# The entry of a fused two-block kernel: modulation by column strips on the tensor engine, and four output groups started quarter by quarter

## The reference, cut to what matters

```python
c_act = jax.nn.silu(c)
mod = c_act @ w_ada[layer] + b_ada[layer]              # 2048 -> 12288
sh1, sc1, gt1, sh2, sc2, gt2 = jnp.split(mod[:, None, :], N_MOD, axis=-1)
h = rmsnorm(x, g_mix[layer]) * (1 + sc1) + sh1
x = x + (1 + gt1) * mixer(h, ...)                      # begins with proj = h @ w_in
h = rmsnorm(x, g_ffn[layer]) * (1 + sc2) + sh2
x = x + (1 + gt2) * conv_ffn(h, ...)
return rmsnorm(x, g_final)
```

## Time and profile before

| what | value |
|---|---|
| median of 3 runs | 2693.53 us (2693.23 to 2693.92) |
| the profiled execution | 2693.06 us |
| its span in the profile | 2691.3 us |
| PE busy | 2606.3 us, 97% of the span |
| DVE busy | 1934.7 us, 72% |
| ACT busy | 1223.7 us, 45% |
| mean granted clock of TensorE | 0.98 |

### The profile page before, as it was taken

How to read it: one execution, slowest core, us unless ns; L and a number is a source line. 1 busy time by engine, 2 the same in 40 slices (tenths; PEclk the granted TensorE clock), 3 DMA queues, 4 the chain that set the end, 5 groups by cost and what they waited for, 6 DMA issues and landing times.

```text
span 2691.3 us, 39482 instructions
## 1 busy us (share of the span) xinstructions
PE 2606.3 (97%) x14717; PEld 2277.7 (85%) x14717; DVE 1934.7 (72%) x2749; ACT 1223.7 (45%) x1595; POOL 118.1 (4%) x177
## 2 busy tenths in 40 slices
PE   5799999999998999999999999998999999999998
PEld 4788888888887888888888888886888888888887
DVE  6987778896888888855666658998676644566554
ACT  2144644444654655544555542004454433444443
POOL 0011121100010000000000000000000000000000
PEclk7699999999999999999999999999999999999999
DMA  9898688875776777755666544552666655666553
GB/s 362 305 299 256 218 249 268 272 222 157 231 259 214 254 247 248 234 188 188 189 189 191 188 158 147 150 155 84 199 180 188 191 189 188 188 188 190 187 185 133
DMA packets 494008, 560.50 MB, mean 208 GB/s; under 512 B 19384, under 2 KB 458937, under 8 KB 493625
## 3 DMA queue, kind: packets, MB, share of 16 engines
q1 hardware_dynamic: 474169, 488.50, 56.5%
q0 software_dynamic: 19712, 70.26, 8.4%
HBM read 553.45 MB, written 2.10 MB: 206 GB/s over the span
## 4 chain that ended last, share of the span: by engine, by line
PE 91%; DVE 5%; DMA 2%; issue 1%; ACT 1%; SPq 0%; ACTq 0%; DVEq 0%
PE ps L1665 53%; PE ps L1667 26%; PE ps L1981 8%; DMA att<-in_w_ada 2%; DVE wlo L976 1%; DVE tCDE L1099 1%; PE ms L1999 1%; PE ms L1716 0%; DVE att L1099 0%; DVE norm_rows L1080 0%; PE ms L1696 0%; PE ms L1739 0%; DVE norm_rows L1015 0%; DVE sq L1554 0%; DVE small L1269 0%
## 5 line engine op out<-in xcount | busy, mean ns | idle before, releaser
L976 DVE TENSOR_TENSOR wlo<-raw,whi 128x1024 fp32r<-128x1024 f32 x794 | 970.6, 1224 | 605.3 <-ACT whi L609 597.3
L1665 PE MATMUL ps<-xhl,whi 128*128 128x512 f32 x4352 | 1381.7, 399 | 16.5 <-DVE xhl L1563 7.3
L609 ACT CAST whi<-raw 128x1024 fp32r<-128x1024 f32 x794 | 831.0, 1050 | 1048.6 <-PE ps L1667 1025.1
L1667 PEld LDWEIGHTS ps<-xhl,wlo 128*128 128x128 f32 x4352 | 823.5, 189 | 195.4
L1667 PE MATMUL ps<-xhl,wlo 128*128 128x256 f32 x4352 | 860.2, 279 | 0.0
L1665 PEld LDWEIGHTS ps<-xhl,whi 128*128 128x128 f32 x4352 | 668.7, 190 | 21.2 <-issue 19.4
L1665 PE MATMUL ps<-ghl,whi 128*128 128x512 f32 x1024 | 319.5, 393 | 0.0
L1667 PEld LDWEIGHTS ps<-ghl,wlo 128*128 128x128 f32 x1024 | 192.2, 188 | 44.5
L1981 PE MATMUL ps<-xg,raw 128*128 128x256 f32 x1024 | 221.3, 379 | 0.0
L1665 PE MATMUL ps<-fhl,whi 128*128 128x512 f32 x704 | 219.3, 393 | 0.0
L1981 PEld LDWEIGHTS ps<-xg,raw 128*128 128x128 f32 x1024 | 194.5, 190 | 26.4
(11 more groups left out here) (263 smaller groups left out, 1447.5 us busy)
## 6 DMA issues: line engine op xcount, KB each, us to landing
raw<-in_w_in SPq DMA_DIRECT2D x176, 512.0 KB, 4.5
raw<-in_w_up SPq DMA_DIRECT2D x176, 512.0 KB, 3.9
ada<-in_w_ada POOLq DMA_DIRECT2D x128, 512.0 KB, 4.7
raw<-in_ffn_w_up SPq DMA_DIRECT2D x128, 512.0 KB, 3.8
raw<-in_ffn_w_down SPq DMA_DIRECT2D x128, 512.0 KB, 3.3
raw<-in_conv_w_pw SPq DMA_DIRECT2D x96, 512.0 KB, 3.8
raw<-in_w_down SPq DMA_DIRECT2D x88, 512.0 KB, 3.4
att<-in_w_ada SPq DMA_DIRECT2D x32, 1024.0 KB, 8.8
```

The source lines that it names most:

```text
L609: nc.scalar.copy(whi[t % SPL][:, :, :], raw[t % RAW][:, :, :]).then_inc(s_hi, 1)
L976: nc.vector.tensor_tensor(wlo[t % SPL][:, :, :], raw[t % RAW][:, :, :], whi[t % SPL][:, :, :].bitcast(F32), ALU.subtract).then_inc(s_lo, 1)
L1665: mm(o[:, m, :, :], whi[t % SPL][:, c, m * P:(m + 1) * P], x, start=first and c == 0, stop=last and c == KC - 1, skip_group_check=True)
L1667: ins = mm(o[:, m, 0, :], wlo[t % SPL][:, c, m * P:(m + 1) * P], x[:, 0, :], start=False, stop=last and c == KC - 1, skip_group_check=True)
```

## The change

Eight modulation groups are now multiplied wholly by PE. `silu(c)` is laid out as 16 blocks of 32 equal columns (`cact_strips`), and chunk j of a piece is multiplied with the block as the stationary operand, its 512 columns moving, into partitions 32j to 32j+31 of a bank: four products that use a quarter of the array's columns each. After four pieces ACT copies the bank (`rows_copied`), and `first_columns` turns it into columns and adds the four strips with a vector that has a one in each strip. DVE does no products any more. The pieces go through a ring of five 1 MB buffers. `x` is loaded first, and its squares are summed in the way of the later norms (`new_square`, `add_older`, `older_sum`, `newest_sum`).

The first 16 units (before: 8) are laid out anew: unit t holds 2 chunks by 512 columns, so that a quarter of four output groups is done as soon as quarter j of `h` is there. A block of a chunk and 256 columns is six products of 256 columns instead of two of 512 and two of 256, all into the same sum, so these four groups need no low copy. The other modulation pieces start later (`pieces_by`), and some background work is moved by four pieces or steps with them.

```diff
+FIRST_RING = 5
+STRIP = 32
+WIDE = 4
+EARLY = 4 * WIDE
+B_ANGLE = 9
...
-    return max(0, s - 2) + (s >= 4) + (s >= 7) + (s >= 10) - sum(s >= B_ROPE + 2 * k for k in range(4))
+    return max(0, s - 8) + sum(s >= 10 + 2 * k for k in range(5)) - sum(s >= B_ROPE + 2 * k for k in range(4))
...
# SP
+            def first_piece(n, q):
+
+                i = 4 * n + q
+                if i >= FIRST_RING:
+                    sp.wait_ge(s_firstmm, i - FIRST_RING + 1)
...
-            for q in (1, 2, 3):
-                first_quarter(0, q)
             x_in = A["x"].rearrange("b (c p) (h t) -> p (b c) h t", p=P, t=T)
...
-            first_quarter(0, 0)
+            for q in range(4):
+                first_piece(0, q)
+            for t in range(2):
+                first_weights(t)
+            first_piece(1, 0)
             sp.dma_start(posi, A["positions"]).then_inc(s_in[1], 16)
             load_vectors(sp, other_vecs, s_vin[1])
             sp.dma_start(cons[:, C_SW128:], A["consts"][:, C_SW128:]).then_inc(s_rest, 16)
+            units_behind = {(1, 3): (2, 3), (2, 3): (4, 5), (3, 3): (6, 7), (5, 1): (8, 9), (5, 3): (10, 11), (7, 1): (12, 13), (7, 3): (14, 15)}
             for n in range(1, ADA_START):
...
+                for q in range(1 if n == 1 else 0, 4):
+                    first_piece(n, q)
+                    for t in units_behind.get((n, q), ()):
+                        first_weights(t)
...
# ACT, after the eight copies of x
+            for i in range(DC // 2):
+                act.wait_ge(s_trx, i + 1)
+                new_square(0, i)
...
+            for t in range(4):
+                split_hi(0, t)
+            rows_copied(0)
...
-                square(i, i)
+            root(0)
...
+            rows_copied(7)
+            first_hi(3)
+            split_hi(0, 14)
+            split_hi(0, 15)
...
+                if t >= EARLY - 2 and t < EARLY:
+                    first_out(2 * (t - EARLY + 2))
...
# DVE
+            for j in range(1, 7):
+                add_older(0, j)
...
+            for t in range(4):
+                split_lo(0, t)
+            read_first(0)
+            root(0, EPS1, s_var2, 1)
+            read_first(1)
+            norm_first(0)
+            for j in range(1, 4):
+                read_first(2 * j)
+                split_lo(0, 4 * j)
+                split_lo(0, 4 * j + 1)
+                read_first(2 * j + 1)
+                norm_first(j)
+                split_lo(0, 4 * j + 2)
+                split_lo(0, 4 * j + 3)
...
# PE
+            def first_piece(n, q):
+
+                i = 4 * n + q
+                pe.wait_ge(s_adaring[i % FIRST_RING], 16 * (i // FIRST_RING + 1))
+                for j in range(4):
+                    ins = mm(row_bank(n)[STRIP * j:STRIP * (j + 1), :], cact_strips[:, 4 * q + j, :], ada_first[i % FIRST_RING][:, j, :],
+                             start=q == 0, stop=q == 3, skip_group_check=True)
+                ins.then_inc(s_firstmm, 1)
+
             def first_columns(n):
+                a = 4 * FIRST[n]
+                pe.wait_ge(s_rows, n + 1)
...
+                for m in range(4):
+                    ins = mm(bank_m[:, a + m:a + m + 1], first_rows[n % 2][:, P * m:P * (m + 1)], one_of_strip[:, 0:1], start=True, stop=True)
...
+            for q in range(4):
+                first_piece(0, q)
+            first_piece(1, 0)
...
-            first_modulation(0)
-            statistic(0)
+            first_columns(0)
             pe.wait_ge(s_posf, 1)
             mm(bank_o[:, T:2 * T], ones[0:1, :], posf, start=True, stop=True).then_inc(s_posb, 1)
+            older_sum(0)
+            newest_sum(0)
+            for q in range(1, 4):
+                first_piece(1, q)
...
+                for m in range(PC):
+                    for x in range(2):
+                        mm(ps[a][:, g, m, :], wh[:, m * P:(m + 1) * P], xhl[:, k, x, :], start=k + x + m == 0, stop=False, skip_group_check=True)
+                for m in range(PC):
+                    ins = mm(ps[a][:, g, m, :], wl[:, m * P:(m + 1) * P], xhl[:, k, 0, :], start=False, stop=k == DC - 1, skip_group_check=True)
...
             for n in range(2, ADA_START):
+                first_piece(n, 0)
+                first_columns(n - 1)
+                first_piece(n, 1)
+                if n >= 3:
+                    first_unit(2 * (n - 3))
+                first_piece(n, 2)
+                if n >= 3:
+                    first_unit(2 * (n - 3) + 1)
+                first_piece(n, 3)
+            first_chunk(10, 0)
+            first_columns(ADA_START - 1)
+            first_chunk(10, 1)
+            first_unit(11)
+            for a in range(2):
+                for g in range(2):
+                    for c in range(2):
+                        ins = first_block(12 + a, c, g)
+                    if g:
+                        ins.then_inc(s_used, 1 + a)
+                    for c in range(2):
+                        ins = first_block(14 + a, c, g)
+                    ins.then_inc(s_firstout, 1)
```

More of the change, by code:

```diff
@@ L98, in nth_split @@
     return t if t < T_PW1 else t - N_PW1
[L101 to L109, removed]
 def pieces_by(s):
-    return max(0, s - 2) + (s >= 4) + (s >= 7) + (s >= 10) - sum(s >= B_ROPE + 2 * k for k in range(4))
+    return max(0, s - 8) + sum(s >= 10 + 2 * k for k in range(5)) - sum(s >= B_ROPE + 2 * k for k in range(4))
 def swap_slot(r):
     return 8 + 2 * (r if r < 8 else r - 4)
-SWAPS_AT = {42: (0, 1), 43: (2, 3), 45: (4, 5), 46: (6, 7), 54: (8, 9), 56: (10, 11)}
+SWAPS_AT = {38: (0, 1), 39: (2, 3), 41: (4, 5), 42: (6, 7), 50: (8, 9), 52: (10, 11)}
 def low_nth(group):
@@ L310, in build @@
         s_cact = sem("c_activated")
-        s_adaring = [None] + [sem(f"first_modulation_landed{s}") for s in range(1, 4)]
+        s_adaring = [sem(f"first_modulation_landed{s}") for s in range(FIRST_RING)]
         s_adaland = [sem(f"modulation_landed{s}") for s in range(2)]
@@ L502, in _ @@
             sp.dma_start(cons[:, C_SW128:], A["consts"][:, C_SW128:]).then_inc(s_rest, 16)
+            units_behind = {(1, 3): (2, 3), (2, 3): (4, 5), (3, 3): (6, 7), (5, 1): (8, 9), (5, 3): (10, 11), (7, 1): (12, 13), (7, 3): (14, 15)}
             for n in range(1, ADA_START):
[L504 to L510, removed]
+                for q in range(1 if n == 1 else 0, 4):
+                    first_piece(n, q)
+                    for t in units_behind.get((n, q), ()):
+                        first_weights(t)
+            columns(EARLY, 24, w_in, 4 * CW)
             w_small = A["w_in"].rearrange("a (h c p) n -> (a h) p c n", p=P, c=DC // 2)
@@ L668, in first_hi, with first_out @@
                     nc.scalar.activation(xh[:, c, :], sq[:, c % 4, :], ACT.Identity, bias=mod[:, c:c + 1]).then_inc(s_nh, 1)
-            root(0)
+            rows_copied(1)
             first_hi(0)
[L672 to L678, removed]
+            rows_copied(2)
+            rows_copied(3)
+            split_hi(0, 4)
+            split_hi(0, 5)
+            first_hi(1)
+            split_hi(0, 6)
+            split_hi(0, 7)
+            rows_copied(4)
+            rows_copied(5)
+            split_hi(0, 8)
+            split_hi(0, 9)
+            first_hi(2)
+            split_hi(0, 10)
+            split_hi(0, 11)
+            rows_copied(6)
+            split_hi(0, 12)
+            split_hi(0, 13)
+            rows_copied(7)
+            first_hi(3)
+            split_hi(0, 14)
+            split_hi(0, 15)
+            act.sem_inc(s_low, WIDE)
+            def first_out(G):
+                act.wait_ge(s_firstout, G + 1)
+                nc.scalar.copy(att[:, 2 * G:2 * G + 2, :], ps[G // 2][:, G % 2, :, :]).then_inc(s_free[G // 2], 1)
             def background(s):
@@ L1774, in first_units @@
-            def first_units(q):
-                for k in range(2):
-                    if q == 0:
-                        pe.wait_ge(s_free[k], 1)
-                    rhs = from_x(H_QKV)
-                    unit(0, 2 * q + k, ps[k], lambda c: rhs(KC * q + c), q == 0, q == 3)
-            for n in range(2, ADA_START):
-                first_columns(n)
-                if n == 7:
-                    first_units(2)
-                first_modulation(n)
-                if n in (4, 5):
-                    first_units(n - 4)
@@ L1789, in _, with first_block @@
-            first_units(3)
+            def first_block(t, c, g):
+                k, a = 4 * (t // 4) + 2 * (t % 4 // 2) + c, t % 2
+                if k == 0 and g == 0:
+                    pe.wait_ge(s_free[a], 1)
+                pe.wait_ge(s_lo, RAW + t + 1)
+                pe.wait_ge(s_h, H_QKV + k + 1)
+                wh, wl = (wide(w[t % SPL])[:, c, CW * g:CW * (g + 1)] for w in (whi, wlo))
+                for m in range(PC):
[3 more added lines that the diff above has]
+                    ins = mm(ps[a][:, g, m, :], wl[:, m * P:(m + 1) * P], xhl[:, k, 0, :], start=False, stop=k == DC - 1, skip_group_check=True)
+                return ins
```

217 lines of the change are left out of this document (87 added, 130 removed).

## The result

The changed kernel takes 2700.86 us (median of 8, 2698.52 to 2704.84) where the one before takes 2693.95 beside it (8 runs, 2692.52 to 2696.43): a ratio of 1.0027, with an interval of 1.0018 to 1.0036. It is slower by some 7 us where 12 less were forecast. The profiled execution took 2701.23 us, its span is 2699.3.

What follows compares the result with a forecast made beforehand. It took the entry as bound by DVE and transfers together, PE mostly idle. 2693.06 - 16.1 (entry) + 3.5 (debts) + 1.0 (clock and strips) = 2681.5; the median 0.5 above, 2682 us; range 2669 to 2697.

Steps and rivals of the forecast that it cites:

- unit 16: End of the entry, from where both kernels issue the same products: PE begins it at 144.0 us, gain 16.1.
- the debts: At the top-64 search, late modulation pieces cost 3.5 us: 2.9 for steps 76 and 77, 0.6 for the next two.
- The transfers: Entry loads: 44.2 MB ahead of the last piece at about 405 GB/s, done at 115.3 us without the hole.
- the clock: Clock falling while PE waits in group 7, with going in and out of strips: 1.0 us lost (0 to 4).
- the strips: Entry pieces: four column strips run at once on PE, 0.86 plus 0.1 us a piece, hidden behind transfers.
- the hole: Near 43 to 50 us the queue empties, piece (2,2) waiting for its buffer: 7.0 us, 3.2 at full clock.
- second: Rival: entry strips overlap only as program order allows, 1.73 us a piece; 2694, no change; chance 0.12.
- third rivals: Rival: entry strips run one after another, 3.45 us a piece, so PE bounds the entry; 2731; chance 0.11.
- fourth rival: PE does not reach full clock from group 3 on: five groups, 35 us, 2717; chance 0.06.
- Steps 78 and 79: Late modulation pieces after the search meet DVE with slack: 0 to 2.9 us, taken as 0.6.
- The bank of unit 16: Unit 16 waits for copies behind the splits of unit 17: from 140.9, 1.04 + 1.22 + 0.6 and delays, to 144.0.
- first rival: Little of the losses comes, in the entry and steps 76 to 79: 2670, or 2676 for half; chance 0.16.

Runs made afterwards that it cites:

- e1: Changed kernel with its new 2-element tile made 128 bytes wide, so later tiles stand on multiples of 64 bytes again: 2694.18 us, ratio 1.0008.
- e2: Changed kernel with its new tile made 64 bytes wide, so later tiles stand on a multiple of 64 but not 128 bytes: 2691.50 us, ratio 0.9995.
- e9: Changed kernel with the new tile allocated last, so every other tile has its address of before: 2688.88 us, ratio 0.9986.
- e3: Kernel before with an unused 2-float tile ahead of `gain2`, moving the tiles behind it by 32 bytes: 2705.52 us, ratio 1.0042.
- e7: Kernel before with unused 2-float tiles ahead of `fhl` and `ghl` only, piece buffers left in place: 2700.25 us, ratio 1.0023.
- e11: Kernel before with an unused tile of 32 elements ahead of `gain2`, moving the tiles behind it by 128 bytes: 2696.53 us, ratio 1.0015.
- e12: Kernel before with `small` and an unused tile allocated ahead of `gain2`, moving the tiles behind by 256 bytes: 2693.32 us, ratio 1.0003.
- e5: Changed kernel with no modulation pieces in steps 73 to 77 and the last one at step 83: 2694.68 us, ratio 1.0005.
- e6: Changed kernel with ACT and DVE emptying the bank of unit 16 before they split units 17 and 18: 2698.73 us, ratio 1.0019.
- e10: Changed kernel with the tile allocated last, hole closed, pieces held back in steps 73 to 77, and bank copies first: 2672.24 us, ratio 0.9922.

## Why the prediction was wrong

**The step that failed** stands in its first paragraph: unit 16, "from where both kernels issue the same products". They are the same products, but not on the same addresses. The sum of the prediction holds no term for the stream behind the entry but the debts, and "The transfers" divides its 44.2 MB by 405 GB/s, the rate of the old addresses. One line of the diff, the new tile of two floats ahead of `gain2`, broke both: 0.03 to 0.04 us on 248 units, some 7 us, and 387 for 405 GB/s, 4.6 to 6.3 us at unit 16. It is shown from both sides, by taking the offset out of the change (e1, e2, e9) and by putting it alone into the kernel before (e3, e7, e11, e12).

**The sum, term by term**, against the profiled 2701.2, 19.7 above the forecast's 2681.5. Unit 16 is 10.9 late (154.87 for 144.0), the search is 2.4 above the 3.5 of the debts, the later units lose 7.2, and the lead shrinks by 0.6 between units 16 and 152. The 1.0 set aside for the clock is in the first of these, and 0.3 comes back behind the last product: 19.8. Of the 10.9, 6.3 go with the offset by the traces of the change and of e9. The other 4.6 are in e9 as well, where addresses are as before: its last piece is used at 126.89 for 123.5 forecast, 3.4 late, and from there to unit 16 it takes 21.7 for 20.5. So the offset was not the only step that failed. Without it the profiled time is 2687.26 (e9), still 5.8 above the forecast: 4.6 at unit 16, of which 1.0 was set aside, 0.7 between there and the search, 2.3 at the search, and nothing in the later units.

**Right: the strips.** "0.86 plus 0.1 for a piece": it is 0.93, and at full clock the pieces are hidden. The second and third rivals fall. The Trainium skill, "TensorE: Matmul & The Clock Gate", "Measured speedup vs the span model", made it 1.1 by three strips at 2.38 times; four strips here come to 3.7 times, an estimate (3.45 / 0.93, where 3.45 is four times the 0.86 of a product alone), better than the page.

**Right: the hole.** Forecast from issue order alone: the queue empty until (2,2) is issued, that piece used at 55.1, 7.0 us lost. It was used at 57.86 and closing the hole brought 8.2 at unit 16 (6.5 against e5). The piece comes 2.8 late, and 2.0 of that are in the first link: unit 3 landed at 42.3 for 40.3, which the lower rate explains in part (13.8 MB at 387 for 405 are 1.6 us).

**Mis-sized: the clock.** "For a clock that falls while PE waits in group 7 ... 1.0 (0 to 4)". In group 6 to 7 PE waited 3.00 us, and from 107.81 to 118.11 it did, for the most part at half clock, what takes 6.01 at full (1.95 from the second piece of the pair at 91.56, at 92.44, to the next at 94.40, and 4.06 from a piece over a unit to the next, as the one that ends at 133.13): 4.3 us. In e9, with 2.57 us of waiting at 102.77, the same work is 3.1 longer; in e5 and e6, with waits of 3.00 and 3.01, it is 3.5 and 2.1 longer, since their granted clock was still 1.00 until 108 us. Behind it PE no longer waits for any piece, so the transfers bound the entry only until 107.8, and not to its last piece as forecast, and what the clock took stayed in the sum. That the wait is what lowers the clock is read from these rows, not tested by itself. The clock had been low once more: behind a wait of 4.33 us before the piece at 65.98 it was 0.50 in the three stretches from 63 to 72 us, past the 70 us that the prediction gave as a sign of being wrong. There PE caught up with the transfers (from 78 to 84 us it was busy for 4.88 of 6 us), so it cost nothing at unit 16 that these rows show. The fourth rival had this mechanism, but for five groups; here it was two, and one of them told.

**Right in place, too small: the debts.** "2.9 for both straight onto the path": PE waited 1.60 and 2.92, together 3.05 more than the 1.47 before the products at 599.11, as the forecast's "some 4 us instead of 1.5" had it. What the prediction lacks is the next link: with 2.92 us of waiting the clock fell, and the next three chunks, from 597.95 to 601.93, took 3.98 us where the kernel before takes 2.17 from 599.42 on, 1.8 less. The lead fell by 5.9 in all; of that 1.0 are in neither, and stay open. Steps 78 and 79, priced at 0.6, can't be told apart in it.

**The small terms.** A chunk of six products took 0.72 us (starts 149.93, 150.65, 151.37 in the timeline) for 0.70: 0.4 us over the last 22 blocks. The bank of unit 16 cost the wait that the prediction priced at "1.04 + 1.22 + 0.6 and some delays": 1.89 us for 1.7. Units on `ghl` take 2.826 us in the change and 2.813 in e3 and e7, at the same address; these 0.013 on 128 units are open. Two figures of the prediction are wrong in themselves and change nothing: by `pieces_by` the kernel before has 11 pieces in steps 9 to 18, not 14, and PE still waited for none of the 15; and the 0.72 for faster exceeds the 0.55 and 0.16 that it is made of.

The first rival, little of the losses, is what e10 reaches by edits: 2672 for its 2670 to 2676.

## What to carry to other kernels

Before you cost the stream behind an edit at nothing, look where the edit puts its new tiles: allocate a small tile last, or pad it so that what stands behind it moves by a multiple that the runs show to be harmless (256 bytes for the transfers here; 64 did for the moving operands), and compare a product's spacing and the GB/s of a filled slice before and after. A wait of about 3 us of PE cost twice here, once as itself and once at half clock behind it (1.8 to 4.3 us more), so price the two together. Follow a load's buffer back through every queue to the instruction that frees it; that gave the hole to within 1.2 us without a run.

## What the runs showed of the hardware that was not expected

- A moving operand 32 bytes past a multiple of 64 costs 2.81 to 2.83 us for four chunks instead of 2.79; 128 bytes of shift (e1) cost nothing, and 64 (e2) make it 2.77.
- An allocation in which the tiles from `gain2` on, the piece buffers among them, are moved by 32, 64 or 128 bytes has its filled queue at 387 GB/s instead of 405 to 409, the same 5% for all three; moved by 256 it loses nothing. The lower rate holds for unit loads too, whose own buffers did not move (384 for 408), and is not there just behind a pause of the queue (411).
- Four column strips of 32-bit products run abreast: 0.93 us for 4 products of 512 columns, each of two records, where one alone is 0.86. The Trainium skill, "TensorE: Matmul & The Clock Gate", "The mechanism", has products start and end in program order across tiles too. Taken as products the strips keep to that: they start 0.006 to 0.007 us apart, in order. It is their records that do not stand as they are issued: both records of a strip are issued together, yet the first records of all four stand within 0.02 us of each other (21.02 to 21.04 us) and the second ones from 21.47 on. The row halves of the earlier trace rows part from the page as products: the second half's product of L1852 starts ahead of the first half's of L1853, which is issued before it.
- After waits of 3.00, 2.57 and 2.92 us the granted clock was 0.50 shortly behind (in e6, with 3.01, it was 1.00 until 109 us, 1.5 us after work began again); after 1.47 and 1.89 us it stayed up. In e10 a wait of 1.92 at 95.19 was followed by a piece of 1.93 us at 98.62, which is the half clock, so the length of one wait does not decide alone.
